# A transformer kernel's first attention: its steps queued ahead of the weight split at the end of a part

## What is computed

```python
proj = h @ w_in                       # q, kc, vc, ks, vs, kw, vw, gates
# per head: three branches, each a masked softmax with a bias per distance
s_c = q . compressed keys + bias      # 15 compressed keys, per group of heads
s   = q . ks + bias                   # selected keys (all blocks are selected at this length)
s_w = q . kw + bias                   # window
o = gate0 * o_c + gate1 * o_s + gate2 * o_w
h = h + o @ w_out
h = h + swiglu(rmsnorm(h))
```

## Time and profile before

| | |
|---|---|
| runs shown | 2122.09, 2122.11, 2123.37 us; median 2122.11 |
| the profiled execution | 2124.48 us, its span 2122.70 us, so 1.78 us lie around the span |
| granted clock of TensorE | 0.998 of full speed over the span |
| busy: PE, weight loads of PE | 2101.6 us (99%), 1808.2 us (85%) |
| busy: DVE, ACT | 1485.0 us (70%), 1057.3 us (50%) |
| stretch of the change | about 185 to 360 us of the span |

### The profile page before, as it was taken

The page is one execution under the profiler, slowest core; times in us unless marked ns, Lnnn a source line. Parts: engine busy times, 40 slices in busy tenths (PEclk is TensorE's granted clock), DMA queues, the critical chain, the costliest instruction groups (busy, mean ns, idle before and its releaser), DMA issues.

```text
span 2122.7 us, 29195 instructions
## 1 busy us (share of the span) xinstructions
PE 2101.6 (99%) x11412; PEld 1808.2 (85%) x11412; DVE 1485.0 (70%) x1985; ACT 1057.3 (50%) x1514; POOL 18.0 (1%) x32
## 2 busy tenths in 40 slices
PE   9999999999999999999999999999999999999998
PEld 7888888888888888888878898888888888888886
DVE  6867665889889787998956676576655565555655
ACT  7654555554444434444455665554443444344443
POOL 1000000000000000000000000000000000000000
PEclk9999999999999999999999999999999999999999
DMA  9785333789989998898955525455555555555553
GB/s 348 252 294 197 120 119 121 297 307 338 342 317 334 351 341 324 321 336 320 358 194 158 205 91 187 170 205 184 191 193 189 198 186 191 198 181 196 193 184 119
DMA packets 73064, 496.16 MB, mean 234 GB/s; under 512 B 8394, under 2 KB 8602, under 8 KB 16352
## 3 DMA queue, kind: packets, MB, share of 16 engines
q1 hardware_dynamic: 69840, 481.20, 62.8%
q0 software_dynamic: 2512, 12.44, 1.6%
q10 hardware_dynamic: 576, 0.66, 0.1%
HBM read 492.09 MB, written 2.16 MB: 233 GB/s over the span
## 4 chain that ended last, share of the span: by engine, by line
PE 93%; ACT 3%; DVE 2%; DMA 2%; issue 1%; SPq 0%; DVEq 0%; ACTq 0%
PE region L1032 40%; PE region L972 30%; PE region L976 15%; PE bank L1113 1%; PE bank L1070 1%; ACT m_WHI L1386 1%; DMA m_RAW<-in_nsa_w_in 1%; PE region L1021 1%; PE bank L1079 1%; PE bank L1011 1%; PE bank L1126 1%; DVE m_WLO L1742 0%; PE region L1022 0%; ACT m_HL L1574 0%; DMA m_RAW<-in_ffn_w_out 0%
## 5 line engine op out<-in xcount | busy, mean ns | idle before, releaser
L1742 DVE TENSOR_TENSOR m_WLO<-m_RAW,m_WHI 128x1024 fp32r<-128x1024 f32 (+3 forms) x729 | 870.0, 1206 | 511.0 <-ACT m_WHI L1386 490.4
L1386 ACT ACTIVATE m_WHI<-m_RAW 128x1024 fp32r<-128x1024 f32 (+3 forms) x729 | 754.0, 1045 | 701.6 <-PE region L1032 375.7
L1032 PE MATMUL region<-m_WHI,m_HL 128*128 128x512 f32 x1152 | 362.5, 396 | 0.6 <-DVE m_HL L1935 0.5
L972 PE MATMUL region<-m_HL,m_WHI 128*128 128x512 f32 x1472 | 357.8, 393 | 0.0
L972 PE MATMUL region<-m_H,m_WHI 128*128 128x512 f32 x1376 | 328.6, 391 | 0.0
L972 PEld LDWEIGHTS region<-m_HL,m_WHI 128*128 128x128 f32 x1472 | 269.4, 188 | 52.1 <-issue 0.3
L972 PEld LDWEIGHTS region<-m_H,m_WHI 128*128 128x128 f32 x1376 | 252.8, 188 | 48.9
L1032 PEld LDWEIGHTS region<-m_WHI,m_HL 128*128 128x128 f32 x1152 | 213.5, 189 | 43.7 <-issue 1.4
L1032 PE MATMUL region<-m_WLO,m_HL 128*128 128x512 f32 x576 | 225.3, 391 | 0.0
L1778 DVE CUSTOM_DVE_ANT_0 m_RAW<-m_RAW,m_CROW,m_consts 128x2048 f32<-128x2048 f32 x96 | 225.1, 2345 | 0.0
L1032 PE MATMUL region<-m_WHI,m_HIDH 128*128 128x512 f32 x512 | 199.2, 389 | 0.0
(11 more groups left out here) (314 smaller groups left out, 1729.2 us busy)
## 6 DMA issues: line engine op xcount, KB each, us to landing
m_RAW<-in_w_ff SPq DMA_DIRECT2D x124, 1024.0 KB, 4.9
m_RAW<-in_w_mod SPq DMA_DIRECT2D x96, 1024.0 KB, 6.5
m_RAW<-in_ffn_w_in SPq DMA_DIRECT2D x88, 1024.0 KB, 6.5
m_RAW<-in_ffn_w_out SPq DMA_DIRECT2D x44, 1024.0 KB, 6.6
m_RAW<-in_nsa_w_in SPq DMA_DIRECT2D x36, 1024.0 KB, 5.5
m_RAW<-in_nsa_w_out SPq DMA_DIRECT2D x16, 1024.0 KB, 4.9
m_RAW<-in_w_out SPq DMA_DIRECT2D x16, 1024.0 KB, 5.0
m_RAW<-in_w_in SPq DMA_DIRECT2D x8, 1024.0 KB, 6.7
```

Of the source, the lines that this page charges most:

```text
L972: mm = e.matmul(region[s["reg"]][:, b, :], hi[:, i, c:c + 128], both[:, k + a + i, :, :].rearrange("p a s -> p (a s)"), start=k + a + i == ...
L1032: mm = e.matmul(o, lhs, rhs, start=start and i == 0, stop=fin and i == 2, skip_group_check=True)
L1386: e.activation(WHI[u % 4][:, 0:(z - a) * ncol], raw[:, a * ncol:z * ncol], ACT.Copy).then_inc(a_hi, 1)
L1742: e.tensor_tensor(WLO[u % 4][:, 0:m], raw[:, a * ncol:z * ncol], WHI[u % 4][:, 0:m].bitcast(F32), ALU.subtract).then_inc(v_lo, 1)
```

## The change

In the stretch in which `flushing` is not empty, the split at the end of a part, which ACT and DVE ran ahead of the steps that `tick()` puts there, is put behind them. Elsewhere the order stays.

```diff
@@ -473,20 +473,25 @@
                 st["parts"] = u + 1
                 for h in flushing:
                     flush(h)
-            if kk == z - 1 and kk < nk - 1:
+            if kk == z - 1 and kk < nk - 1 and not flushing:
                 split()
             if st["owed"] and kk % 2 == 0 and s["arg"] == 1:
                 st["owed"] -= 1
                 split()
             if kk < nk - 1 and (s["groups"] is not WIDE or kk % 2) and s["groups"] is not CMP:
                 tick()
+            if kk == z - 1 and kk < nk - 1 and flushing:
+                split()
         flush_later()
         if last:
             finish_slab(s)
-        split()
+        if not flushing:
+            split()
         if last and s["kind"] in ("glu", "relu"):
             put("hid", s["i"])
         tick()
+        if flushing:
+            split()
         if every:
             u = every.pop(0)
             if u is not None:
```

## The result

The changed kernel takes 2125.12 us (median of 20 runs, 2123.84 to 2129.07), the kernel before 2122.44 us in the same comparison (median of 20, 2120.59 to 2125.55). The ratio is 1.0016, 95% interval 1.0009 to 1.0022: slower by 3.4 us, between 1.9 and 4.7 (the two medians by themselves lie 2.68 us apart). So there is a loss that is clear of the noise, and its middle value is smaller than the 0.2% that the prediction calls "the same". The profiled execution of the changed kernel took 2124.71 us, its span is 2122.9 us. In the changed kernel every line behind the edit is numbered 5 higher: 1070, 1079, 1203, 1210, 1386, 1742 of before are 1075, 1084, 1208, 1215, 1391, 1747.

What follows compares the result with a forecast made beforehand. PE was taken as the bound. The terms 0.3 + 1.31 + 1.34 - 0.82 + 1.2 sum to +3.33 us, giving 2125.4 us from the profiled execution set to the median 2122.11; range 2120.8 to 2129.0, about 0.83.

Steps and rivals of the forecast that it cites:

- a): Group 0, scores 2: split 85 on ACT waits for the copy of cturn 0, so soft1 0 starts later; +0.3 us.
- b): Group 0, turn 1 1: splits 87 on DVE and 88 on ACT delay the copy of turn 1 0; +1.31 us.
- c): Group 0, cscore 1: DVE's half of split 88 waits for ACT's, and feat 14 comes late; +1.34 us.
- d): Groups 1 and 2 up to 290 us: DVE catches up and no step comes later than PE asks; 0.
- e): Turn 8 1, at 291.54 us: PE's wait for the copy of turn 8 0 goes away; -0.82 us.
- f): Cturn 3: split 107 behind soft2 11 on ACT delays DVE's cscore 3, so PE waits; +1.2 us.
- Only the gain: Rival: ACT and DVE absorb the new waits and the wait at 291.54 goes; 2121.3 us, chance 0.18.
- no effect: Rival: everything stays hidden over the whole kernel; 2122.1 us, chance 0.04.
- Slower beyond the noise: Rival: b and c's price recurs in group 1 or 2, 2128.1 us, chance 0.17; in both, 2130.7, chance 0.06.
- No wait for `WHI` or `WLO`: Rival weights late: a late DVE half makes PE wait for these, 2 to 4 us more, 2128.5; chance 0.04.
- The full 4.19 us: Rival: measurably faster, all that PE's weight-load busy time allows in the attention; 2117.9 us, chance 0.01.
- The view that could mislead: PE's weight-load busy time in the attention allows 4.19 us of gain, against 2.0 by the list of waits, which decided.

Runs made afterwards that it cites:

- e3_dve_only: The changed kernel with ACT's half of every split back at its old place, so only DVE's half goes late; 2120.84 us, 0.9997 of the kernel before.
- e1_group0: The kernel before with the new order only for splits 79 to 90, group 0; 2125.83 us, ratio 1.0014 to the kernel before.
- e6_only105: The kernel before with only split 105 put behind its steps; 2121.19 us, ratio 0.9994 to the kernel before.
- e7_105_86: The kernel before with split 105 behind its steps and split 86 behind scores 1 and soft1 1; 2120.46 us, ratio 0.9988 to the kernel before.
- e5_keep107: The changed kernel with split 107 left at its old place ahead of its steps; 2123.54 us, ratio 1.0003 to the kernel before.
- e4_act88_89_early: The changed kernel with ACT's halves of splits 88 and 89 alone at their old places; 2122.65 us, ratio 1.0003 to the kernel before.
- e10_dve_from91_86: The kernel before with split 86 behind scores 1 and soft1 1, and DVE's half alone late from split 91 on; 2120.29 us, ratio 0.9994.
- e8_dve_only_86: Meant to add split 86's move to DVE's halves alone late; as built split 86 stayed, repeating that order; 2121.40 us, 0.9997 of the kernel before.

## Why the prediction was right

The forecast, 2125.4 us, was the likeliest case and the measured median is 2125.12; the range 2120.8 to 2129.0 holds it. Its sum was +3.33. The stretch has +2.48, the runs +3.4 (1.9 to 4.7). That the two medians agree to 0.3 us is luck: the sum is 0.85 too high for the stretch, the base, 2122.11, was 0.33 below the median of before in the comparison, and a ratio is known to some 1.4 us here. What holds is the list of places and their prices. By its steps:

- **Two waits become four**, at the lines named (1075, 1084, 1208, 1215 after), and the one near 291 us is gone: all as told.
- **a)** +0.3 forecast, +0.28 measured. The copy of cturn 0 at 197.45 holds up split 85, which starts at 197.73, 0.44 later than before once the 0.48 is taken off (197.73 - 0.48 - 196.81). The wait at scores 2 grew from 1.22 to 1.51. In e3_dve_only, where ACT does split 85 at its old place, it is 1.2.
- **b)** +1.31 forecast, +1.24 measured. The copy of turn 1 0 was walked to 216.73 and came at 217.12 - 0.48 = 216.64. The wait in the list is 1.06, less than the delay of 1.24. Read a delay from start times, not from the wait in front of it: the ends of matmuls are modelled.
- **c)** +1.34 forecast, +1.26 measured; 1.15 in the list.
- **d)** 0 forecast, -0.27 measured, all of it between `cscore 2` and cturn 2 (264.86 to 270.06 before, 268.14 to 273.05 after: 5.20 and 4.91 us). The walk looked there for losses alone and missed a gain. The timeline of before at this place:

```profile
266.06 1.22 DVE L1742 TENSOR_TENSOR m_WLO<-m_RAW,m_WHI 128x1024 fp32r<-128x1024 f32 x1 [1.34 <-ACT m_WHI L1386]
...
267.20 0.37 DVE L1837 TENSOR_TENSOR m_Pc<-bank,m_biasA 128x28 f32<-128x28 f32 x2
```

  DVE's softmax of `cscore 2` starts behind a split, 2.34 after the matmuls of `cscore 2`; after the change 1.16 (269.30 less 268.14). So cturn 2 came to PE a little late before, by an amount that the list of waits doesn't name. The interval is 5.20 in e1_group0, e6_only105 and e7_105_86, where this split keeps its old place, and 4.91 or 4.92 in the seven other experiments, in which DVE's half is late.
- **e)** -0.82 forecast, -1.12 measured (cturn 2 to `cscore 3`: 36.17 before, 35.05 after). With split 105 alone moved, in e6_only105, it is 35.22, so 0.95 is the wait of the list, which shows 0.82 of it, and 0.17 comes from other splits in between. No run took these apart.
- **f)** +1.2 forecast, +1.19 measured; e5_keep107 shows that split 107 is the cause, by 1.20.
- The sum of the misses in d, e and the end of the stretch (-0.27, -0.30, -0.10) is 0.67 of the 0.85 us between forecast and stretch. So the mechanism held, and the terms mis-sized are the gains, each too small.
- **Cause.** For b the prediction named two things: split 87 on DVE ahead of soft1 2, and split 88 on ACT between soft2 2 and the copy. e4_act88_89_early shows that the second is 0.95 of the 1.24 us; by e3_dve_only the first costs 0.24. For c the reason was that DVE's half waits for an ACT half that is stuck behind soft2. That is shown by both: with ACT's half early 1.26 us shrink to 0.05 or less.
- **The chances.** The four cases that the range is said to hold add up to 0.89 (0.50, 0.18, 0.04 and 0.17), not 0.83; the prediction doesn't say what it took off.
- **The rivals.** "Only the gain" and "no effect" fell: the interval lies above 1 and b and c are there. "Slower beyond the noise" needed one more wait in group 1 or 2, and there is none. No wait for `WHI` or `WLO` appeared between 180 and 380 us, and the one listed at line 1032, 0.4 us behind 1000 us, is in before and after alike. The full 4.19 us was not the change's to give.
- **The view that could mislead.** The busy time of PE's weight loads allowed 4.19 us of gain, the list of waits 2.0. e10_dve_from91_86 got 2.55 and no listed wait is left. So the list, by which the prediction decided, was short by 0.55. The Trainium skill (Perfetto Trace Analysis, Identifying the Most-Contended Engine) prefers the busy share of weight loads to that of matmuls; here that view lay 1.64 above what the best order tried could reach. The 4.19 rests on the rate of another stretch with another mix of matmuls and loads, as the prediction said, so this doesn't show the measure itself to be wrong.
- **A sign of error that misled.** The prediction said that it would be wrong altogether if the time behind 380 us changed by more than a few tenths. In the two profiled executions it does, by 2.5 us (2.98 at 1003 us, 0.44 at 1097), though not through the change: it was a longer pause behind a load, and slower matmuls behind that, in the one execution of before. The eleven other executions scatter by 2.0 us there, so one profile of each is too few for that test.

## What to carry to other kernels

A piece of work without a deadline that stands in an in-order queue ahead of an instruction that has to wait anyway cost nothing here. Put behind that instruction it delayed all that followed; and as two engines shared the piece, the second waited for the first (2.88 and 2.94 us) and what was queued behind it was late as well. So move such a piece on the one engine, and at the one place, where it stands ahead of what the busiest engine waits for (here split 86 and split 105, and from split 91 on DVE's halves but not ACT's), and check it by walking each queue with the durations of the trace: the walk gave four delays of 0.3 to 1.3 us to within 0.1. When the largest gain open is a fifth of a per cent, read it from marks within the trace, since whole runs scatter by as much.

## What the runs showed of the hardware

In the execution of before the granted clock fell behind the late load. Windows there (the column behind POOL's busy time is the granted clock):

```profile
1064.00:1066.00 2.00, 0.34 (x2) 0.00 (x0) 2.00 (x4) 1.00 (x3) 0.00 (x0) 1.00 0.91 380
1066.00:1068.00 2.00, 1.62 (x10) 1.48 (x11) 0.23 (x1) 1.88 (x7) 0.00 (x0) 0.85 0.16 66
1068.00:1070.00 2.00, 2.00 (x6) 1.59 (x5) 1.01 (x1) 2.00 (x4) 0.00 (x0) 0.50 0.01 4
1070.00:1072.00 2.00, 2.00 (x8) 1.60 (x8) 1.35 (x2) 1.54 (x5) 0.00 (x0) 0.80 0.38 70
```

PE had stood still for 2.04 us until 1066.38. The clock then falls to 0.50, the level of 1.2 GHz, and is back at 2.4 GHz after 1072 us. What these three windows lack of the full clock is 0.15, 0.50 and 0.20 of 2 us each, 1.70 us by this estimate, so the lower clock accounts for the 1.60 us by which the 120 matmuls behind took longer (28.83 us against 27.23 to 27.25 in the eleven other executions).

It is tempting to say that a pause of 2 us brings the lower clock. The other traces don't bear this out. In e8_dve_only_86 PE stood still at the same place for as long, 2.09 us, and the clock stayed at 1.00:

```profile
1066.08 1.06 PE L1142 MATMUL bank<-m_ident,m_XG 128*128 128x128 f32 x8 [2.09 <-DVE m_XG L1977]
```

```profile
1066.00:1068.00 2.00, 1.92 (x13) 1.76 (x14) 0.00 (x0) 1.88 (x7) 0.00 (x0) 1.00 0.51 213
1068.00:1070.00 2.00, 2.00 (x11) 1.63 (x10) 1.30 (x2) 2.00 (x4) 0.00 (x0) 1.00 0.00 0
```

Pauses of 2.17 us (e6_only105) and 2.32 us (e8_dve_only_86) near 46 us left it at 1.00 too, as did the 1.10 us of after at 1068 us and the waits of 1.51 and 1.22 us in the stretch of the change. So a pause of 2.04 us was followed by the lower clock in one of twelve executions, and why there and not behind the equal or longer ones stays open.
